# A hybrid RWKV-7, Hyena and PEER layer: the gate matrix of the dense tiles in three parts of 56, 16 and 56 blocks instead of four of 32, and eight first-layer blocks beside its first part

## The chip, the cores and the metric

One core of one Trainium2 chip runs the whole layer in one launch. The metric is the device time in microseconds (us), the median of repeated runs of the same program. In the text PE is TensorE, DVE is VectorE, ACT is ScalarE, POOL is GpSimd and SP is SyncE; "L1061" is line 1061 of the kernel before.

## The reference, cut to what matters

One layer of width D = 1024 on 128 context tokens and 512 latent tokens: modulation from `w_ada` (six parts), a mixer (combined projection `w_in`, low-rank "LoRA" products for decay, rate and gate, scans, long convolutions, `w_out`), and then PEER experts, all in float32:

```
def peer(h):                       # for all 640 tokens, 8 heads, top 16 of 16384 experts each
    q = (x @ peer_wq).reshape(T, 8, 2, 128)
    s = einsum('thpd,phkd->thpk', q, peer_keys)        # scores against 2 x 128 keys
    sv, si = top_k(s, 16)
    cand = sv[:, :, 0, :, None] + sv[:, :, 1, None, :]
    cidx = si[:, :, 0, :, None] * 128 + si[:, :, 1, None, :]
    top_s, pos = top_k(cand.reshape(T, 8, 256), 16)
    eidx = take_along_axis(cidx..., pos)               # 8 x 16 = 128 experts per token
    gate = softmax(top_s)
    act = gelu(einsum('cd,ced->ce', x, u_tab[eidx])) * gate
    return einsum('ce,ced->cd', act, v_tab[eidx])
x = x + gate2 * peer(h);  y = rmsnorm(x, final_norm)
```

`u_tab` and `v_tab` have 16384 rows of 1024 floats, 67 MB each.

## The kernel before, in words

**Start.** The weights `w_ada`, `w_in`, `w_out` and `peer_wq` come in chunks of 2 MB that SP issues into a ring of three slots (`WBUF` = 3), in the order of `WCH` (four `ada` chunks, one `in`, two `ada`, then mostly `in`). PE's modulation products (L544) take one `ada` chunk each. Five loads of the LoRA weights stand before the third chunk (`if n == 2`); what they bring is used by the LoRA products in the mixer, after the first `w_in` products.

**Tiles.** The 640 tokens are five tiles of 128. Each token of tile 0 (context) and of latent tiles 1 and 2 gets its 128 expert rows of `u` and of `v` by indirect DMA, one per slot (128 partitions of 1024 floats, 0.524 MB). Tile 0 is done before the stretch that the change is about. For tiles 1 and 2 there are `ROWS` = 512 such gathers, issued by POOL (L2213) into a ring of `RING` = 8 and consumed in order by DVE: a `u` row by one operation that forms the dot products (L2036), a `v` row by one that adds it to the sum (L2041). POOL waits until DVE has given a slot back.

**Dense tiles.** The last two latent tiles (`ND` = 256 tokens) are computed against all 16384 experts, in `ETILES` = 128 blocks of 128 experts. Per block i:

- SP loads `u` block i (three buffers) once `hidden(i - 3)` is done, and `v` block i (two buffers) once `back(i - 2)` is done, 0.524 MB each.
- PE `hidden(i)` (L1061, 16 records of 128x256): expert activations from the `u` block, into one of two PSUM banks.
- ACT takes the gelu of it to one of four buffers `sgel` (L1389).
- DVE `weigh(i)` multiplies it by row i of the gate matrix (L2080).
- PE `back(i)` (L1072, 8 records of 128x512) adds its product with the `v` block to the output in PSUM.

**The gate matrix** `gmat` holds, for a block and a token, the gates of the 128 experts of the block. It is built from one-hot vectors, for 8 tokens at a time (a group; `GROUPS` = 32 groups per part), and for `QI` = 32 blocks at a time (a part; `NPART` = 4). For a group, DVE makes three arrays: `one_j` (L2068, 1024 bf16 elements a partition), `same_i` (L2071, 8 per block of the part) and `one_i` (L2073, 24 per block of the part). PE multiplies them, 24 matmuls (L1083), and ACT copies the result to `gmat` (L1397), which has two halves of 32 rows. One-hots and PSUM have two buffers. The first part stands before block 2's `hidden`; the groups of each further part are spread over the 28 steps after its predecessor's start, by `groups_by(i)`.

**Order.** Each engine runs its own list, written out by hand, with semaphores between them. PE's list:

```
hidden(0); hidden(1)
... transposes of the slots and gates of the dense tiles ...
for g in range(GROUPS): gate_group(g)
for i in range(2, ETILES):
    hidden(i); back(i - 2); the gate groups due by groups_by(i - 2)
```

DVE's step i is: `weigh(i)`, the one-hots due, a piece of the top-k of tile 1 or 2 (`FIRST_STEPS`: the first stage; `ROUTE_STEPS`: the routing, whose end releases that tile's gathers on POOL through `eid_ok`), and the gathered rows due by `rows_by(i)`: 400 over the steps 12 to 95, then 112 over the steps 95 to 126. After step 127 come the final sums and norms (`fin_*`).

**Ahead of block 0.** The top-k of the two dense tiles (t = 3 and 4) runs on DVE, with an exponential on ACT (`route_exp`) that waits for DVE's routing. ACT copies the tokens `h2` of the gathered tiles (L1380), and PE's transposes wait for those copies (L1049). PE then spreads the output gate `gate2` over the partitions (`spread`, L726; ACT's copy `g2bc`, L1382), which is used first when the final sums of the tiles are made (steps 104 and 108).

Of the kernel before, what the change touches and what calls it, by code (L numbers as in the profile page):

```python
# [71 lines left out]
QI = 32  # L72
GROUPS = ND // GRP
NPART = NKEY // QI
# [55 lines left out]
def program(nc, a, outs):  # L130
# [5 lines left out]
    with ExitStack() as ctx:  # L136
# [136 lines left out]
        gmat = at(SB - 2 * QI * ND, 2 * QI, ND)  # L273
# [7 lines left out]
        g2bc = pr(2, D)  # L281
        sc_a = at(g2bc.offset, 4, 2, NKEY)
# [10 lines left out]
        keyN = at(cand.offset, 2 * EXPH, NKEY)  # L293
        sv = tk(NLT, 2 * EXPH, TOPK)
# [25 lines left out]
        one_i = [half(hr(3 * QI * GRP // 2), 3, QI, GRP) for _ in range(2)]  # L320
        same_i = half(hr(QI * GRP // 2), 1, QI, GRP)
        iota8 = half(hr(P * GRP // 2), 1, P, GRP)
        slot5 = half(hr(5 * ND // 2), 5, 2, P)
        junk = hr(D).bitcast(mybir.dt.bfloat16).rearrange("p (a b) -> p a b", b=D)
# [5 lines left out]
        yo = [at(gmat.offset + (NT + 1 + t if t < 2 else QI * ND // D + t - 2) * D, D) for t in range(NT)]  # L330
# [39 lines left out]

        block = ctx.enter_context(nc.Block())
# [3 lines left out]
        def _(sp):  # L375
# [135 lines left out]
            for i in range(ETILES):  # L511
                if i + UB < ETILES:
                    sp.wait_ge(S("s_mm"), i + 1)
                    load_u(i + UB)
                if i >= 2 and i - 2 + VB < ETILES:
                    sp.wait_ge(S("v_mm"), i - 1)
                    load_v(i - 2 + VB)
                if i == 100:
                    sp.wait_ge(S("x_out"), 16)
                    sp.wait_ge(S("xc_out"), 16)  # L520
                    sp.wait_ge(S("a_ok"), (NPART - 1) * QI)
                    sp.dma_start(xr, spill).then_inc(S("ld_xr"), 16)
                    sp.dma_start(fnorm, a["final_norm"].partition_broadcast(P)).then_inc(S("ld_xr"), 16)
# [8 lines left out]
        def _(pe):  # L532
# [531 lines left out]
            def back(i):  # L1064
# [3 lines left out]
                if i == 0:  # L1068
                    pe.wait_ge(S("gate_ok"), 3)
                for r in range(2):  # L1070
                    for c in range(2):
                        m = pe.matmul(ps[:, 2 * r + c, :], sgel[:, i % SBUFS, P * r:P * r + P], vs[i % VB][:, 512 * c:512 * c + 512],  # L1072
# [3 lines left out]
            def gate_group(g):  # L1076

                pe.wait_ge(S("one_ok"), g + 1)
                if g >= 2:
                    pe.wait_ge(S("g_ev"), g - 1)  # L1080
                for c in range(GRP):
                    for k in range(3):
                        m = pe.matmul(ps[:, 6 + g % 2, QI * c:QI * c + QI], one_j[:, g % 2, :, c], one_i[g % 2][:, k, :, c],  # L1083
# [28 lines left out]
        def _(act):  # L1112
# [257 lines left out]
            for n in range(4 * EXPH):  # L1370
                q_out(n)
                for t in (3, 4):
                    if n == ROUTE_AT[t]:
                        route_exp(t - 1)
# [6 lines left out]
            act.wait_ge(S("gate_mm"), 3)  # L1381
            own.do(A(g2bc[:, :, :].rearrange("p c n -> p (c n)"), ps[:, 0:4, :].rearrange("p a b -> p (a b)"), ACT.Copy), S("gate_ok"))  # L1382

            def gelu_out(i):

                act.wait_ge(S("s_mm"), i + 1)
                if i >= SBUFS:
                    act.wait_ge(S("v_mm"), i - SBUFS + 1)
                A(sgel[:, i % SBUFS, :], ps[:, 4 + i % 2, 0:ND], ACT.Gelu).then_inc(S("gel_ok"), 1)  # L1389

            def gates_out(g):
# [3 lines left out]
                if q >= 2:  # L1395
                    act.wait_ge(S("a_ok"), QI * (q - 1))
                A(gmat[:, QI * (q % 2):QI * (q % 2) + QI, GRP * k:GRP * k + GRP], ps[:, 6 + g % 2, 0:QI * GRP].rearrange("p (t i) -> p i t", i=QI),  # L1397
                  ACT.Copy).then_inc(S("g_ev"), 1)

# [16 lines left out]
            for g in range(GROUPS):  # L1416
                gates_out(g)
            ng, ne, nr = 2, GROUPS, 4
            for i in range(ETILES):
                while ng < min(i + 3, ETILES):  # L1420
                    gelu_out(ng)
                    while ne < groups_by(ng - 2):
                        gates_out(ne)
                        ne += 1
                    ng += 1
# [21 lines left out]
        def _(dve):  # L1447
# [577 lines left out]
            def gather_row(n):  # L2025
# [9 lines left out]
                if e == 0:  # L2035
                    V.scalar_tensor_tensor(junk[:, m % 2, :], slot, 1.0, h2[:, 1 + t, :], ALU.mult, ALU.mult,  # L2036
# [24 lines left out]
            def one_hots(g):  # L2061
# [67 lines left out]
            dve.wait_ge(S("gate_ok"), 3)  # L2129
# [16 lines left out]
            for i in range(ETILES):  # L2146
# [10 lines left out]
                for k, t in enumerate((1, 2)):  # L2157
# [7 lines left out]
                    if i == lo:  # L2165
                        parts[t] = route_tile(t)
# [125 lines left out]
```

## Time and profile before

| | |
|---|---|
| median of the runs | 2684.29 us (2683.68, 2684.29, 2685.72) |
| profiled execution, its own time | 2703.06 us |
| its span, from first to last instruction | 2701.2 us |
| mean granted clock of TensorE | 0.933 of full speed |
| busy: PE | 2391.4 us (89%) |
| busy: PE weight loads | 1674.8 us (62%) |
| busy: DVE | 1794.5 us (66%) |
| busy: ACT | 495.1 us (18%) |
| busy: POOL | 937.1 us (35%) |
| read from HBM | 635.5 MB |

The profile is of one execution, and all times of the trace count from the start of its span. An engine's busy time says how much of the span it worked, not whether it set the pace; for that the span has to be taken stage by stage, and the waits in a stage read. A granted clock of 1 is 2.4 GHz, of 0.5 is 1.2 GHz; a mean between them says for what share of a stretch each held. A release behind `<-` names what ended the idle time before an instruction.

### The profile page before, as it was taken

The numbers are of one execution on the slowest core, as the hardware profiler recorded it, in microseconds if no ns is written. First come the engines' busy times: TensorE is split into PE (matmuls) and PEld (weight loads), VectorE is DVE, ScalarE is ACT, GpSimd is POOL, SyncE is SP. The second block draws the span as 40 slices with busy tenths as digits, with TensorE's granted clock in tenths as the row PEclk, the third lists the DMA queues.
The fourth block names the chain that finished last, engine by engine and source line by source line (L and its number), as shares of the span: only waits on it lengthen the run. The fifth ranks groups of instructions, "written<-read, shape, count | busy, mean of one in ns | idle before, by whom it ended". The sixth has DMA issues, their size and how long they took to land.

```text
span 2701.2 us, 43634 instructions
## 1 busy us (share of the span) xinstructions
PE 2391.4 (89%) x18034; PEld 1674.8 (62%) x18034; DVE 1794.5 (66%) x3466; ACT 495.1 (18%) x1002; POOL 937.1 (35%) x774
## 2 busy tenths in 40 slices
PE   5989978788788878999879899998999899998997
PEld 2545536667777766334468787775776567775664
DVE  0111253335677776577689795799899888886767
ACT  2111124224344332100122210100000100000101
POOL 0000000000144442155441000667766567765653
PEclk8999988998899998899999769999999899999999
DMA  9233031130166665287886013999999999999997
GB/s 299 94 131 118 5 135 41 56 103 2 47 227 188 218 197 180 86 313 251 309 329 227 17 48 129 346 406 384 409 407 395 337 409 392 409 407 411 409 409 301
DMA packets 199455, 647.01 MB, mean 240 GB/s; under 512 B 25222, under 2 KB 27142, under 8 KB 198298
## 3 DMA queue, kind: packets, MB, share of 16 engines
q0 software_dynamic: 110592, 402.70, 39.8%
q1 hardware_dynamic: 88666, 241.52, 24.2%
q8 instruction: 143, 2.34, 0.4%
q14 instruction: 54, 0.44, 0.0%
HBM read 635.50 MB, written 8.65 MB: 238 GB/s over the span
## 4 chain that ended last, share of the span: by engine, by line
PE 55%; DVE 14%; DMA 13%; issue 6%; POOL 5%; ACT 4%; another core or an unknown queue 1%; SPq 1%; DVEq 0%; POOLq 0%; ACTq 0%
DMA arena<-in_peer_v,arena 8%; PE ps L1061 7%; PE ps L595 7%; PE ps L1072 7%; PE ps L1083 5%; POOL arena L2213 4%; DMA arena<-in_peer_u,arena 3%; PE ps L1037 3%; PE ps L829 3%; PE ps L987 2%; PE ps L1002 2%; DVE arena L2041 2%; PE ps L597 2%; PE ps L835 1%; DMA arena<-in_w_in 1%
## 5 line engine op out<-in xcount | busy, mean ns | idle before, releaser
L1072 PE MATMUL ps<-arena 128*128 128x512 f32 x1024 | 473.3, 606 | 45.2 <-DVE arena L2080 40.5
L1061 PE MATMUL ps<-arena 128*128 128x256 f32 x2048 | 480.2, 388 | 1.6 <-issue 1.6
L2213 POOL DMA_INDIRECT arena<-in_peer_u,arena x256 | 339.7, 1327 | 380.3 <-DVE arena L1832 231.9
L1061 PEld LDWEIGHTS ps<-arena 128*128 128x128 f32 x2048 | 392.1, 195 | 70.8 <-issue 21.3
L2213 POOL DMA_INDIRECT arena<-in_peer_v,arena x256 | 306.2, 1196 | 193.8 <-DVE arena L2041 141.3
L2041 DVE SCALAR_TENSOR_TENSOR arena<-arena 128x1024 f32<-128x1024 f32 x252 | 316.1, 1284 | 83.9 <-DMA arena<-in_peer_v,arena 77.1
L2201 POOL DMA_INDIRECT arena<-in_peer_u,arena x128 | 147.5, 1153 | 614.6 <-DVE arena L1832 335.4
L1072 PEld LDWEIGHTS ps<-arena 128*128 128x128 f32 x1024 | 196.1, 194 | 252.2 <-issue 241.4
L2036 DVE SCALAR_TENSOR_TENSOR arena<-arena 128x1024 bf16<-128x1024 f32 x256 | 304.1, 1223 | 46.6 <-DMA arena<-in_peer_u,arena 41.1
L1083 PEld LDWEIGHTS ps<-arena 128*128 128x128 bf16 x3072 | 207.2, 157 | 51.0 <-issue 47.0
L1083 PE MATMUL ps<-arena 128*128 128x32 bf16 x3072 | 210.3, 243 | 4.3 <-DVE arena L2073 4.1
L595 PE MATMUL ps<-arena 128*128 128x512 f32 x384 | 182.9, 632 | 20.2 <-DMA arena<-in_w_in 17.9
L2201 POOL DMA_INDIRECT arena<-in_peer_v,arena x128 | 140.5, 1098 | 172.7 <-DVE arena L1869 137.2
L1500 DVE SCALAR_TENSOR_TENSOR arena<-ps,arena 128x504 f32<-128x504 f32 x48 | 35.7, 743 | 242.3 <-ACT arena L1159 241.4
L829 PE MATMUL ps<-arena 64*64 64x128 f32 x1920 | 189.0, 282 | 8.0 <-ACT arena L1289 7.1
L1865 DVE SCALAR_TENSOR_TENSOR arena<-arena 128x1024 bf16<-128x1024 f32 x128 | 154.3, 1223 | 57.2 <-DMA arena<-in_peer_u,arena 56.8
L1869 DVE SCALAR_TENSOR_TENSOR arena<-arena 128x1024 f32<-128x1024 f32 x126 | 155.8, 1284 | 1.6 <-DMA arena<-in_peer_v,arena 1.0
L1389 ACT ACTIVATE arena<-ps 128x256 f32<-128x256 f32 x128 | 48.9, 383 | 554.8 <-PE ps L1061 464.0
L595 PEld LDWEIGHTS ps<-arena 128*128 128x128 f32 x384 | 76.1, 204 | 112.7 <-issue 88.6
L1397 ACT ACTIVATE arena<-ps 128x256 f32<-128x256 f32 x128 | 49.1, 384 | 473.6 <-PE ps L1083 452.1
L2191 POOL MEMSET arena<- 128x1024 f32 x1 | 1.0, 951 | 372.5 <-PE ps L614 372.5
L829 PEld LDWEIGHTS ps<-arena 64*64 64x64 f32 x1920 | 108.5, 139 | 27.4 <-issue 15.3
(354 smaller groups left out, 3431.2 us busy)
## 6 DMA issues: line engine op xcount, KB each, us to landing
arena<-in_uT SPq DMA_DIRECT2D x128, 512.0 KB
arena<-in_peer_v SPq DMA_DIRECT2D x128, 512.0 KB
arena<-in_w_ada SPq DMA_DIRECT2D x12, 2048.0 KB, 18.1
arena<-in_peer_wq SPq DMA_DIRECT2D x12, 2048.0 KB, 9.5
arena<-in_w_in SPq DMA_DIRECT2D x6, 2048.0 KB, 8.1
arena<-in_w_out SPq DMA_DIRECT2D x4, 2048.0 KB, 8.0
arena<-in_peer_u,arena POOLq DMA_INDIRECT x384
arena<-in_peer_v,arena POOLq DMA_INDIRECT x384
```

Of the source, the lines that this page charges most:

```text
L595: pe.matmul(ps[:, n % 2, :], w[:, k, P * f:P * f + P], hT[:, k, LC:T], start=(k == 0), stop=(k == KD - 1))
L829: m = pe.matmul(xo[r, u, :, i, :], nT[r, :], zz[r, h // 2, 0:2, i, :], start=False, stop=(l == LEVELS - 1), skip_group_check=True)
L1037: m = pe.matmul(ps[:, n % 2, 0:ND], ring[slot_of["wq", j]][:, k, P * f:P * f + P], half[:, k, :], start=(k == 0), stop=(k == KD - 1))
L1061: m = pe.matmul(ps[:, 4 + i % 2, 0:ND], us[i % UB][:, k, :], hTd[:, k, :], start=(k == 0), stop=(k == KD - 1))
L1072: m = pe.matmul(ps[:, 2 * r + c, :], sgel[:, i % SBUFS, P * r:P * r + P], vs[i % VB][:, 512 * c:512 * c + 512], start=(i == 0), stop=(i == ...
L1083: m = pe.matmul(ps[:, 6 + g % 2, QI * c:QI * c + QI], one_j[:, g % 2, :, c], one_i[g % 2][:, k, :, c], start=(k == 0), stop=(k == 2))
L1865: m = V.scalar_tensor_tensor(junk_c[c % 2], slot, 1.0, h2_c, ALU.mult, ALU.mult, accum_out=dots_c[:, m:m + 1])
L1869: m = V.scalar_tensor_tensor(dst, slot, coef_c[:, m:m + 1], dst, ALU.mult, ALU.add)
L2036: V.scalar_tensor_tensor(junk[:, m % 2, :], slot, 1.0, h2[:, 1 + t, :], ALU.mult, ALU.mult, accum_out=dots[:, m:m + 1]).then_inc(S("g_used ...
L2041: V.scalar_tensor_tensor(acc[:, m % 2, :], slot, coef[:, m:m + 1], acc[:, m % 2, :], ALU.mult, ALU.add).then_inc(S("g_used"), 1)
L2201: pool.indirect_dma_start(gring_c[k], None, a[("peer_u", "peer_v")[e]][0], bass.IndirectOffsetOnAxis(ap=ids_c[:, m:m + 1], axis=0)).then_i ...
L2213: pool.indirect_dma_start(gring[:, n % RING, :], None, a[("peer_u", "peer_v")[e]][0], bass.IndirectOffsetOnAxis(ap=ids[:, t, m:m + 1], axi ...
```

## The change

- The gate matrix is built in three parts, of 56, 16 and 56 blocks, in a `gmat` of 72 rows. A group of the first and third part has 56-block one-hots, so 24 matmuls of 56 columns. The second part's groups are due one a step from step 18 on, the third part's 32 groups in the 15 steps from 55.
- `hidden(0)` and `hidden(1)` stand where they did; `hidden(2)` to `hidden(7)` stand among the groups of the first part, after groups 4, 9, 14, 19, 24 and 29, on PE and ACT alike. The first four gelu results stay in rows 56 to 59 of `gmat`, which the second part fills later. SP loads the first `u` blocks accordingly.
- The routing of tile 1 takes the steps 4 to 10 (before: 4 to 12), that of tile 2 the steps 44 to 54 (44 to 58). The gathered rows are due from step 10 on, 400 over 85 steps, and the last 112 over 28 steps instead of 31.
- The exponential of tile 4's routing stands behind ACT's `h2` copies. The spreads of `gate2` and their copies move from before block 0 to the steps 96 and 98.
- The LoRA loads stand before the ninth weight chunk instead of the third.
- Buffers move with it: the dot operation's full-size result goes over its ring slot (before: `junk`), `sc_a` to `cand`, `g2bc` and `yo` to rows of `gmat`. `xr` is loaded after 96 weighings, as before.

```
-QI = 32
-NPART = NKEY // QI
+PARTS = ((0, 56), (56, 16), (72, 56))
+GROWS = 72
+FRONT = 4
+AHEAD = FRONT + SBUFS
+AHEAD_AT = {4: 2, 9: 3, 14: 4, 19: 5, 24: 6, 29: 7}
 def rows_by(i):
-    return max(0, min(EARLY, (i - 12) * EARLY // 83)) + max(0, min(ROWS - EARLY, (i - 95) * (ROWS - EARLY) // 31))
+    return max(0, min(EARLY, (i - 10) * EARLY // 85)) + max(0, min(ROWS - EARLY, (i - 95) * (ROWS - EARLY) // 28))
 def groups_by(i):
-    return min(NPART * GROUPS, GROUPS + GROUPS * (i // QI) + min(GROUPS, (i % QI + 1) * 8 // 7))
+    if i < 56:
+        return GROUPS + max(0, min(GROUPS, i - 17))
+    return min(3 * GROUPS, 2 * GROUPS + (i - 55) * GROUPS // 15)
-ROUTE_STEPS = {1: (4, 12), 2: (44, 58)}
-ROUTE_AT = {3: 2 * EXPH + 10, 4: 2 * EXPH + 15}
+ROUTE_STEPS = {1: (4, 10), 2: (44, 54)}
+ROUTE_AT = 2 * EXPH + 10
...
+        def sg(i):
+            return front[:, i, :] if i < FRONT else sgel[:, i % SBUFS, :]
...
-                if n == 2:
+                if n == 8:
                     for d in range(2):
                         sp.dma_start(lora1[...])
...
-            for i in range(ETILES):
-                if i + UB < ETILES:
+            for i in range(AHEAD):
+                sp.wait_ge(S("s_mm"), i + 1)
+                load_u(i + UB)
+            for i in range(2, ETILES):
+                if AHEAD <= i < ETILES - UB:
                     sp.wait_ge(S("s_mm"), i + 1)
                     load_u(i + UB)
-                if i >= 2 and i - 2 + VB < ETILES:
+                if i - 2 + VB < ETILES:
                     sp.wait_ge(S("v_mm"), i - 1)
                     load_v(i - 2 + VB)
...
-            for c in range(2):
-                m = spread(40, c, 2 * c)
-            m.then_inc(S("gate_mm"), 1)
...
             for g in range(GROUPS):
                 gate_group(g)
+                if g in AHEAD_AT:
+                    hidden(AHEAD_AT[g])
             ng = GROUPS
             for i in range(2, ETILES):
-                hidden(i)
+                if i >= AHEAD:
+                    hidden(i)
                 back(i - 2)
                 while ng < groups_by(i - 2):
                     gate_group(ng)
                     ng += 1
+                if i in (96, 98):
+                    pe.wait_ge(S("g_ev"), 3 * GROUPS)
+                    pe.wait_ge(S("gate_ok"), 2 + (i - 96) // 2)
+                    spread(40, (i - 96) // 2, 6).then_inc(S("gate_mm"), 1)
...
-            act.wait_ge(S("gate_mm"), 3)
-            own.do(A(g2bc..., ps[:, 0:4, :]..., ACT.Copy), S("gate_ok"))
+            route_exp(3)
...
+                if q == 1:
+                    act.wait_ge(S("v_mm"), FRONT)
+                if q == 2:
+                    act.wait_ge(S("a_ok"), w)
...
-                dve.wait_ge(S("g_ev"), GROUPS * (i // QI + 1))
+                dve.wait_ge(S("g_ev"), GROUPS * (part_of(i) + 1))
```

## Rows read from the trace of the kernel before

**Rows 1.** The page: GB/s in 40 slices; the gathers' queue (packets, MB, share)
```profile
GB/s 299 94 131 118 5 135 41 56 103 2 47 227 188 218 197 180 86 313 251 309 329 227 17 48 129 346 406 384 409 407 395 337 409 392 409 407 411 409 409 301
...
q0 software_dynamic: 110592, 402.70, 39.8%
```

**Rows 2.** Stage table: stretch, length, busy PE PEld DVE ACT POOL, clock, DMA, GB/s
```profile
1535.00:1595.00 60.00, 58.28 (x785) 54.73 (x786) 51.87 (x126) 12.43 (x33) 0.00 (x0) 0.52 0.01 2
1764.60:2446.00 681.40, 653.53 (x3598) 463.35 (x3596) 606.69 (x1106) 61.16 (x156) 462.74 (x363) 0.98 1.01 396
2446.00:2680.70 234.70, 217.67 (x736) 139.51 (x736) 167.07 (x160) 19.33 (x40) 130.72 (x110) 0.99 1.02 407
1981.90:2117.10 135.20, 123.42 (x686) 85.63 (x687) 132.59 (x217) 10.73 (x28) 78.70 (x66) 0.95 0.96 373
2079.90:2220.00 140.10, 123.92 (x602) 83.93 (x601) 125.69 (x160) 12.36 (x28) 86.72 (x73) 0.93 0.96 369
```

**Rows 3.** Timeline of PE at the start: start, us, instruction, idle time and releaser
```profile
22.20 1.92 PE L544 MATMUL ps<-arena 128*32 128x512 f32 x16 [1.75 <-DMA arena<-in_w_ada]
...
35.28 3.64 PE L544 MATMUL ps<-arena 128*32 128x512 f32 x16 [10.17 <-DMA arena<-in_w_ada]
...
41.07 3.47 PE L544 MATMUL ps<-arena 128*32 128x512 f32 x16 [0.35 <-DVE arena L1477]
```

**Rows 4.** Timeline of PE, from the h2 transposes to the first groups
```profile
1518.26 1.97 PE L1049 MATMUL ps<-arena 128*128 128x128 f32 x8 [8.46 <-ACT arena L1380]
...
1520.02 4.79 PE L726 MATMUL ps<-arena 128*128 128x128 f32 x32
1524.64 7.07 PE L1061 MATMUL ps<-arena 128*128 128x256 f32 x32
1535.54 26.06 PE L1083 MATMUL ps<-arena 128*128 128x32 bf16 x384 [3.17 <-DVE arena L2073]
```

**Rows 5.** Timeline: one group's operations on DVE, and hidden(2) behind the first part
```profile
1560.98 0.69 DVE L2068 TENSOR_TENSOR arena<-arena 128x1024 bf16<-128x1024 bf16 x1
1561.59 0.28 DVE L2071 TENSOR_TENSOR arena<-arena 128x256 bf16<-128x256 bf16 x1
1561.91 0.56 DVE L2073 TENSOR_TENSOR arena<-arena 128x768 bf16<-128x768 bf16 x1
1562.38 0.68 DVE L2068 TENSOR_TENSOR arena<-arena 128x1024 bf16<-128x1024 bf16 x1
...
1588.49 6.36 PE L1061 MATMUL ps<-arena 128*128 128x256 f32 x16
```

**Rows 6.** Timeline of PE at block 8; then the chain of waits at block 3
```profile
1648.91 3.06 PE L1083 MATMUL ps<-arena 128*128 128x32 bf16 x48
1651.79 5.38 PE L1061 MATMUL ps<-arena 128*128 128x256 f32 x16
```
```profile
1599.83 3.51 PE ps L1061 x16
1603.33 3.43 PE ps L1072 x8
```

**Rows 7.** Stage table of tile 4's routing and of a first stage; the first gather
```profile
1491.10:1517.10 26.00, 18.07 (x99) 15.97 (x97) 25.30 (x87) 4.16 (x16) 0.00 (x0) 0.90 0.00 0
1590.90:1596.20 5.30, 5.30 (x16) 3.82 (x15) 5.16 (x34) 0.38 (x1) 0.00 (x0) 0.72 0.10 19
```
```profile
1683.14 1.12 POOL L2213 DMA_INDIRECT arena<-in_peer_u,arena  x1 [231.90 <-DVE arena L1832]
```

**Rows 8.** Timeline: the ninth gather, and five rows of v on DVE
```profile
1708.81 1.68 POOL L2213 DMA_INDIRECT arena<-in_peer_u,arena  x1 [15.48 <-DVE arena L2036]
...
2119.08 6.09 DVE L2041 SCALAR_TENSOR_TENSOR arena<-arena 128x1024 f32<-128x1024 f32 x5
```

**Rows 9.** Waits from 1524 to the end: who, for whom: us, times, longest
```profile
DVE arena L2068 <- PE ps L1083: 49.6, 28, 7.0
```

**Rows 10.** Timeline of PE: the last block's back product
```profile
2682.59 5.37 PE L1072 MATMUL ps<-arena 128*128 128x512 f32 x8 [3.51 <-DVE arena L2080]
```

More of the change, by code:

```diff
@@ L71 @@
 UB, VB, SBUFS, GRP = 3, 2, 4, 8
-QI = 32
 GROUPS = ND // GRP
-NPART = NKEY // QI
+PARTS = ((0, 56), (56, 16), (72, 56))
+GROWS = 72
+WIDEST = max(w for _, w in PARTS)
+FRONT = 4
+AHEAD = FRONT + SBUFS
+AHEAD_AT = {4: 2, 9: 3, 14: 4, 19: 5, 24: 6, 29: 7}
 ROWS = (GT - 1) * 2 * SLOTS
@@ L319, in program @@
         one_j = half(hr(2 * P * GRP // 2), 2, P, GRP)
-        one_i = [half(hr(3 * QI * GRP // 2), 3, QI, GRP) for _ in range(2)]
-        same_i = half(hr(QI * GRP // 2), 1, QI, GRP)
+        one_at = [hr(3 * WIDEST * GRP // 2).offset for _ in range(2)]
+        one_i = [[half(at(o, 3 * w * GRP // 2), 3, w, GRP) for o in one_at] for _, w in PARTS]
+        same_at = hr(WIDEST * GRP // 2).offset
+        same_i = [half(at(same_at, w * GRP // 2), 1, w, GRP) for _, w in PARTS]
         iota8 = half(hr(P * GRP // 2), 1, P, GRP)
         slot5 = half(hr(5 * ND // 2), 5, 2, P)
-        junk = hr(D).bitcast(mybir.dt.bfloat16).rearrange("p (a b) -> p a b", b=D)
         us = [at(x.offset + i * D, KD, P) for i in range(UB)]
@@ L329, in program @@
         fnorm = at(gmat.offset + NT * D, D)
-        yo = [at(gmat.offset + (NT + 1 + t if t < 2 else QI * ND // D + t - 2) * D, D) for t in range(NT)]
+        yo = [at(gmat.offset + n * D, D) for n in (6, 14, 7, 8, 9)]
+        g2bc = at(gmat.offset + 15 * D, 2, D)
+        front = gmat[:, 56:56 + FRONT, :]
         ring_at = SB - WBUF * KD * 512
@@ L1080, in gate_group @@
                     pe.wait_ge(S("g_ev"), g - 1)
+                w = PARTS[g // GROUPS][1]
                 for c in range(GRP):
                     for k in range(3):
-                        m = pe.matmul(ps[:, 6 + g % 2, QI * c:QI * c + QI], one_j[:, g % 2, :, c], one_i[g % 2][:, k, :, c],
+                        m = pe.matmul(ps[:, 6 + g % 2, w * c:w * c + w], one_j[:, g % 2, :, c], one_i[g // GROUPS][g % 2][:, k, :, c],
                                       start=(k == 0), stop=(k == 2))
@@ L1371, in _ @@
                 q_out(n)
-                for t in (3, 4):
-                    if n == ROUTE_AT[t]:
-                        route_exp(t - 1)
+                if n == ROUTE_AT:
+                    route_exp(2)
             sc_out(4 * EXPH - 1)
@@ L1380, in _ @@
                 own.do(A(h2[:, 1 + i // 2, 512 * (i % 2):512 * (i % 2) + 512], ps[:, 4 + i % 2, :], ACT.Copy), S("h2_ok"))
-            act.wait_ge(S("gate_mm"), 3)
-            own.do(A(g2bc[:, :, :].rearrange("p c n -> p (c n)"), ps[:, 0:4, :].rearrange("p a b -> p (a b)"), ACT.Copy), S("gate_ok"))
+            route_exp(3)
             def gelu_out(i):
                 act.wait_ge(S("s_mm"), i + 1)
-                if i >= SBUFS:
+                if i >= AHEAD:
                     act.wait_ge(S("v_mm"), i - SBUFS + 1)
-                A(sgel[:, i % SBUFS, :], ps[:, 4 + i % 2, 0:ND], ACT.Gelu).then_inc(S("gel_ok"), 1)
+                A(sg(i), ps[:, 4 + i % 2, 0:ND], ACT.Gelu).then_inc(S("gel_ok"), 1)
             def gates_out(g):
@@ L1394, in gates_out, with gate_out @@
                 q, k = divmod(g, GROUPS)
-                if q >= 2:
-                    act.wait_ge(S("a_ok"), QI * (q - 1))
-                A(gmat[:, QI * (q % 2):QI * (q % 2) + QI, GRP * k:GRP * k + GRP], ps[:, 6 + g % 2, 0:QI * GRP].rearrange("p (t i) -> p i t", i=QI),
+                lo, w = PARTS[q]
+                row = lo % GROWS
+                if q == 1:
+                    act.wait_ge(S("v_mm"), FRONT)
+                if q == 2:
+                    act.wait_ge(S("a_ok"), w)
+                A(gmat[:, row:row + w, GRP * k:GRP * k + GRP], ps[:, 6 + g % 2, 0:w * GRP].rearrange("p (t i) -> p i t", i=w),
                   ACT.Copy).then_inc(S("g_ev"), 1)
+            def gate_out(c):
+                act.wait_ge(S("gate_mm"), 3 + c)
+                own.do(A(g2bc[:, c, :], ps[:, 6:8, :].rearrange("p a b -> p (a b)"), ACT.Copy), S("gate_ok"))
             def fin_square(t):
@@ L2035, in gather_row @@
                 if e == 0:
-                    V.scalar_tensor_tensor(junk[:, m % 2, :], slot, 1.0, h2[:, 1 + t, :], ALU.mult, ALU.mult,
+                    V.scalar_tensor_tensor(slot.bitcast(mybir.dt.bfloat16)[:, 0:D], slot, 1.0, h2[:, 1 + t, :], ALU.mult, ALU.mult,
                                            accum_out=dots[:, m:m + 1]).then_inc(S("g_used"), 1)
@@ L2165, in _ @@
                     if i == lo:
+                        rown.settle()
                         parts[t] = route_tile(t)
```

32 lines of the change are left out of this document (19 added, 13 removed).

## The prediction

> **What bounds the kernel now.** The page's slices come first: from the 26th on they move about 350 to 410 GB/s, most of them 409, while those from the 23rd to the 25th move 17 to 129 [rows 1]. The stage table splits that end [rows 2]; its edges are DVE's weighings of a block (the records of line 2080, counted). Between those of block 20 (1764.6) and block 95 (2446.0) DMA moves 396 GB/s, PE is busy 653.5 of 681.4 us and DVE 606.7. From 2446.0 to the last gathered row DMA moves 407 GB/s. So the last 1000 us are bound by bytes, with PE and DVE close behind. What comes before them is a chain in which DMA is almost idle: 1535 to 1595 moves 2 GB/s, with TensorE's clock at 0.52, that is mostly 1.2 GHz [rows 2]. A microsecond saved ahead of the first gather at 1683.14 [rows 7] starts the byte-bound stretch earlier; one of PE saved inside it saves nothing unless PE was the one that was late.
>
> **The start: the five LoRA loads go from before the third weight chunk to before the ninth.** PE waits 10.17 us for the third `w_ada` chunk, to 35.28, because SP issues it behind them [rows 3]. Without them it follows the second chunk, which was there at 22.2. A chunk is 2.1 MB, 5.1 us at 409 GB/s, so it lands at about 27.3. The fourth needs the slot of the first, long free then, and lands at 32.5; PE began on it at 41.07 [rows 3]. That is 8.5 us at the fourth chunk; I take 8, since PE idles twice there and may run it at the half clock. What follows, to the scores, is a chain that shifts as it stands. The loads now queue behind the second `w_in` chunk, for which PE waits too, but behind it in the same queue: 0 (at worst their 1.6 MB share with it, 4 us). **-8** (bounds -9 and -3).
>
> **Between scores and gate matrix.** PE idles 8.46 us for ACT's first copy of `h2`, which stands behind the exponential of tile 4's routing, then runs the 32 matmul records of the two `g2bc` spreads (4.79 us), then `hidden(0)` and `hidden(1)` (7.07), and the first group starts at 1535.54 [rows 4]. After the change the exponential stands behind the copies and the spreads are gone from here. The copies and transposes run at 1510 to 1513 and the two blocks to 1520, beside the routing, whose end on DVE (the exponential waits for it at 1517.1 [rows 7]) is then no longer what they wait for. From the end of `hidden(1)` to the first group the index transposes, ACT's copies and `split_gates` take the 3.8 us of now, or a little more, as ACT loads its gelu table there: 1524.3 instead of 1535.5. **-11** (bounds -12 and -7). The spreads come back at blocks 96 and 98, where PE has slack under the bytes: 0.
>
> **The first part of the gate matrix.** Now its 32 groups take 53.0 us (1535.5 to 1588.5), 1.63 each on PE (26.06 us for 384 matmuls) at the half clock [rows 4, 5]. DVE's three one-hot operations start 0.61, 0.32 and 0.47 us apart; they take 0.69, 0.28 and 0.56 us for 1024, 256 and 768 elements, 0.53 ns an element [rows 5]. With 56 blocks they have 1024, 448 and 1344: 0.61 + 0.42 + 0.78 = 1.81 us a group, 58 in all. On PE a group becomes 24 matmuls of 56 columns, which no row shows. From below it is the 32-column group at full clock, 1.53 us [rows 6], from above that in proportion to the columns, 2.7. I take 1.5 at full and up to 1.8 at half clock: 32 columns took 1.53 and 1.63 at the two clocks, so it is not the columns that they wait for. The Trainium skill, in "TensorE: Matmul & The Clock Gate", Back-to-back issue gap, prices 1 to 64 columns alike, by which 56 columns cost what 32 do; no run here has 56, and by the upper bound the first and the third part would cost PE some 37 us more each.
>
> Six `hidden` blocks now stand among these groups, one after every fifth. Behind 3.06 us of groups alone the block at 1651.79 took 5.38 us instead of 3.51, and the one behind the whole part 6.36 [rows 4, 5, 6]: groups bring the clock down, and a block behind them starts at 1.2 GHz. Each of the six has 9 us of groups before it, so I take 6.1 each, 36.6 in all; at full clock they would be 21. The opening is 58 + 36.6, less 1.6 that DVE gets ahead: 93 us, from 1524.3 to 1617. **+40 on the opening, +29 at its end.**
>
> **From there to the first gather.** Now 94.6 us (1588.5 to 1683.1), paced by PE steps of 3.51 + 3.43 + 1.5 = 8.4 us [rows 6], since every step holds a hidden block, a back block and a group that DVE's one-hots wait for. After the change PE has no groups before step 18 and only back blocks for steps 2 to 7, so DVE sets the pace: 1 us to the first weighing, four steps of 0.33 for the weighing and 5.2 for the first stage of four score rows (22.1), then the routing, 26.0 us when nothing disturbs it [rows 7]. Its heavy operations come in steps 8 and 9. Step 8 needs `hidden(8)`: weighing 4, two backs, one hidden, 23.4 + 10.4 = 34 us; from there DVE's step 8 takes 12 and step 9 six. **52 us**: the first gather at 1669.5, not 1683.1, -13.6.
>
> **The byte-bound stretch.** A row and a block of u or v are 0.524 MB each (402.7 MB are 768 gathers [rows 1]). Now DVE frees the first slot of the ring of 8 only 25.7 us after the first gather (1708.81); POOL stands 15.48 us for it [rows 7, 8]. After the change rows are due from step 11, and 42 before step 20; with 20 blocks of u and v that is 32.5 MB, 79.5 us at 409 GB/s, and 6 for landing and coupling: block 20 at 1755 (now 1764.6). Steps 20 to 95 hold 6.71 transfers each against 6.82: 8.58 us, 643.8 in all, against 655. Now they take 681.4, 26 over: 6.5 in steps 24 to 31 (9.54 each), 13 in 44 to 57 (135.2 us, DVE busy 132.6 [rows 2]), 7 spread. A row costs DVE 1.22 us (five in 6.09 [rows 8]). After:
> - 24 to 31: DVE has 5.74 rows + 0.33 + 1.25 (a 16-block group) + 1.72 (first stage: what 9.54 leaves now) = 9.04: +3.7.
> - 44 to 54: DVE 63.2 rows + 3.6 + 7.5 + 26 + 1 = 101.3 against 94.4: +6.9.
> - 55 to 69: the third part's 32 groups in 15 steps. PE 6.94 + 2.13 x 1.5 = 10.1; DVE 5.74 + 0.33 + 2.13 x 1.81 = 9.9. I take 10.3: +25.8.
> - spread: +7.
>
> That is 687.2, so block 95 at 2442 against 2446. The fourth part's groups, 1.5 us on PE and 1.4 on DVE each, leave engines that wait for bytes there: 0. From 95 on 112 rows, 56 blocks and 3.1 MB of residual are 91.2 MB, 223 us, + 4 as now (234.7 for 94.3 MB [rows 2]): last row at 2669, not 2680.7. The rows now end at step 123. Behind them stand, on PE alone, back(124), hidden(127) and three backs, 4 x 3.43 + 3.51 + 1.4 = 18.6, then the 13.2 us that follow the last back now [rows 10]: 2700.8. Against 2701.2: **-0.4**. So the 13.6 us ahead of the gather and the fuller start behind it are nearly all given back, to the crowded third part and the longer tail.
>
> **Sum.** -8 - 0.4: the span goes from 2701.2 to 2692.8, the profiled execution from 2703.06 to 2694.7. The median of the runs is 2684.29, 18.8 lower; the difference carried over unchanged gives **2676**.
>
> **Rivals.** (a) *The clock stays up in the opening.* For it: 56 columns stream 1.75 times as long as 32 in a group. Against it: the two blocks of rows 5 and 6. Then the six blocks cost 3.5 each and all 15 us are saved ahead of the gather: 2661. [...]
> (b) *The third part crowds out the rows; slower than before.* In steps 55 to 69 PE takes a group only when DVE has made it, and DVE makes one only when PE has taken the one two before; each has 10 us of work a step. Now DVE waits 28 times for PE's groups, up to 7.0 us [rows 9]. If the two alternate, one group's 1.5 + 1.8 us no longer overlap, a step is up to 12.2 us and DMA runs at under 330 GB/s. From 1.3 us a step over my 10.3 the saving is gone; at 11.7 (+21) it is 2697. For it: in 2079.9 to 2220 steps are 9.34 us at 369 GB/s [rows 2] with half the groups. Against it: DVE's stretch 1981.9 to 2117.1, busy 132.6 of 135.2, shows no such waiting.
> (c) *The start doesn't carry.* If the LoRA loads hold up `w_in`, or a later load takes the 8 us back, the dense part's nothing is left: 2684.
>
> **Chances.** Forecast 0.40, (a) 0.15, (b) 0.33, (c) 0.12. 0.2% (5.4 us) is about what a measurement can tell. The forecast's own range is 2667 to 2685: 0.27 faster, 0.11 same, 0.02 slower. (a) is 0.15 faster; (b) 0.26 slower, 0.07 same; (c) 0.06 faster, 0.06 same. Together 0.48, 0.24, 0.28. The range runs from below (a) to above (b)'s middle: 2655 to 2701.
>
> **What would show it.** In the profile after: the third `w_ada` wait ending near 27; the first group at 1516; six `hidden` blocks of 5.2 to 6.9 us among groups, and a clock near 0.6 there; DVE's groups 1.8 us apart; the first gather near 1661; steps 55 to 69 at 10.3 us with DMA near 340 GB/s; 70 to 95 at 8.6 with DMA at 409; 32 us from the last row to the end. It is wrong if 56-column groups take much over 1.5 us at full clock, if the six blocks take 3.5, if steps of the third part pass 11.5, or if the spread losses of 20 to 95 go or double, since I carried them over.

## The result, and the profile after

The kernel after takes 2766.5 us (median of 4 runs, 2763.5 to 2767.8), the kernel before beside it 2685.0: a ratio of 1.031, 95% interval 1.029 to 1.032. A later set of runs, with the kernel before at 2703.9, gave 1.030 (1.027 to 1.033). It is 3% slower, where 0.3% faster was forecast, and lies outside the forecast's range of 2655 to 2701 us. Two of the ten executions of e3 below took 3432 and 3918 us, and its ratio is that of the other eight. The profiled execution took 2763.5 us, its span is 2761.6.

Two lines of the page after, the granted clock and the GB/s by slices of 69 us:

```profile
PEclk9999979889899998999998689999999889999999
GB/s 270 118 180 61 61 114 2 89 65 2 128 223 192 221 222 46 309 265 261 369 276 23 25 83 359 409 370 404 409 358 328 248 246 345 409 409 411 408 408 241
```

Against [rows 1] one hole is new: the 31st to 33rd slices move 328, 248 and 246 GB/s, where they moved 395, 337 and 409 before. The stage table after, with the columns of [rows 2], cut at the first group, the first weighing, the first gather, the blocks 20, 55, 73 and 95, and the start of the last gathered row's operation:

```profile
1497.84:1614.20 116.36, 115.71 (x864) 109.47 (x864) 58.11 (x97) 19.83 (x38) 0.00 (x0) 0.68 0.09 28
1614.20:1666.50 52.30, 46.60 (x129) 25.37 (x130) 49.67 (x227) 1.15 (x3) 0.02 (x1) 0.94 0.34 115
1666.50:1753.40 86.90, 83.06 (x320) 54.62 (x318) 57.11 (x103) 7.65 (x16) 59.43 (x49) 0.98 1.01 398
1753.40:2069.70 316.30, 292.55 (x1548) 201.79 (x1548) 290.25 (x596) 24.81 (x69) 202.23 (x165) 0.98 0.99 388
2069.70:2304.30 234.60, 234.60 (x1215) 184.74 (x1213) 166.20 (x239) 24.37 (x50) 107.04 (x84) 0.88 0.74 271
2304.30:2496.10 191.80, 161.40 (x545) 101.70 (x544) 135.17 (x223) 9.76 (x24) 135.42 (x105) 0.98 1.03 409
2496.10:2727.50 231.40, 207.62 (x704) 131.25 (x703) 163.76 (x156) 19.97 (x40) 125.92 (x111) 0.99 1.01 401
```

In the fifth stage PE is busy 234.60 of 234.60 us and DVE 166: these are the steps with the third part's groups. Before, the blocks 55 to 73 took

```profile
2079.90:2248.60 168.70, 152.52 (x770) 104.91 (x769) 149.51 (x205) 15.04 (x35) 105.70 (x85) 0.93 0.96 370
```

The timeline of PE shows what the opening and that stage consist of (start, us, instruction):

```profile
1497.84 13.20 PE L1096 MATMUL ps<-arena 128*128 128x56 bf16 x120 [4.25 <-DVE arena L2106]
1510.86 5.35 PE L1075 MATMUL ps<-arena 128*128 128x256 f32 x16
1516.05 13.14 PE L1096 MATMUL ps<-arena 128*128 128x56 bf16 x120
...
2134.02 3.60 PE L1084 MATMUL ps<-arena 128*128 128x512 f32 x8
2137.45 5.35 PE L1096 MATMUL ps<-arena 128*128 128x56 bf16 x48
2142.62 5.21 PE L1075 MATMUL ps<-arena 128*128 128x256 f32 x16
```

L1096 is the gate group (L1083 before), L1075 `hidden` and L1084 `back`. Five groups of 56 columns take 13.20 us, 2.64 each, where 32 columns took 1.63 [rows 4] and I had put 1.5 to 1.8. Two of them in a step take 5.35. Stage rows of single stretches: groups alone in the third part, the `hidden` block behind them, and groups alone in the opening:

```profile
2124.00:2128.90 4.90, 4.90 (x48) 4.90 (x47) 1.85 (x3) 0.55 (x1) 1.55 (x2) 0.98 1.00 388
2129.00:2131.50 2.50, 2.50 (x8) 2.06 (x7) 2.27 (x4) 0.54 (x1) 0.00 (x0) 0.50 0.90 365
1498.00:1510.80 12.80, 12.80 (x120) 12.80 (x120) 8.86 (x15) 2.19 (x4) 0.00 (x0) 0.50 0.00 1
```

The granted clock is 0.98, 0.50 and 0.50. The first and the third row are groups alone, so a matmul of 56 columns costs about 110 ns at 1.2 and at 2.4 GHz alike. It is not TensorE's own speed that it waits for. The second row belongs to a `hidden` block behind a pair of groups, which takes 5.2 us, where one behind a single group of the second part takes 3.70. That part's groups, with 16 columns, are the cheap ones (1.58 us for 24 matmuls):

```profile
1757.45 1.58 PE L1096 MATMUL ps<-arena 128*128 128x16 bf16 x24
1758.88 3.70 PE L1075 MATMUL ps<-arena 128*128 128x256 f32 x16
```

### The profile page after: what moved, and what is told of

It is laid out like the page before. It is cut to its first block, busy times and chain, and to the rows that moved or that the text cites. A ratio compares the mean times of both kernels' runs of the same rounds, so it can differ in the third digit from the quotient of the medians.

```text
span 2761.6 us, 41938 instructions
## 1 busy us (share of the span) xinstructions
PE 2439.6 (88%) x17266; PEld 1707.7 (62%) x17266; DVE 1773.6 (64%) x3370; ACT 491.8 (18%) x971; POOL 919.2 (33%) x774
## 4 chain that ended last, share of the span: by engine, by line
PE 45%; DMA 20%; DVE 18%; issue 7%; POOL 5%; ACT 3%; SPq 0%; DVEq 0%; POOLq 0%; ACTq 0%
DMA arena<-in_peer_v,arena 9%; DMA arena<-in_peer_u,arena 9%; PE ps L613 7%; PE ps L1096 6%; PE ps L1075 6%; PE ps L1084 4%; POOL arena L2248 4%; PE ps L1005 2%; PE ps L1020 2%; PE ps L847 2%; PE ps L615 2%; DVE arena L1743 1%; DVE arena L2073 1%; POOL arena L2236 1%; DVE arena L1901 1%
## 5 line engine op out<-in xcount | busy, mean ns | idle before, releaser
L1084 PE MATMUL ps<-arena 128*128 128x512 f32 x1024 | 480.0, 614 | 89.8 <-DVE arena L2113 88.3
L1075 PE MATMUL ps<-arena 128*128 128x256 f32 x2048 | 502.2, 402 | 0.7 <-issue 0.7
L2248 POOL DMA_INDIRECT arena<-in_peer_u,arena x256 | 331.0, 1293 | 421.3 <-DVE arena L1864 239.5
L1075 PEld LDWEIGHTS ps<-arena 128*128 128x128 f32 x2048 | 412.7, 204 | 90.8 <-issue 34.9
L1084 PEld LDWEIGHTS ps<-arena 128*128 128x128 f32 x1024 | 194.1, 196 | 315.6 <-issue 311.2
L2248 POOL DMA_INDIRECT arena<-in_peer_v,arena x256 | 299.0, 1168 | 237.7 <-DVE arena L2073 180.6
L2068 DVE SCALAR_TENSOR_TENSOR arena<-arena 128x1024 bf16<-128x1024 f32 x256 | 308.1, 1223 | 89.3 <-DMA arena<-in_peer_u,arena 87.6
L2236 POOL DMA_INDIRECT arena<-in_peer_u,arena x128 | 146.1, 1142 | 602.9 <-DVE arena L1864 335.6
L1096 PEld LDWEIGHTS ps<-arena 128*128 128x128 bf16 x2304 | 219.7, 153 | 29.6 <-issue 29.1
L1096 PE MATMUL ps<-arena 128*128 128x56 bf16 (+1 forms) x2304 | 220.6, 263 | 4.2 <-DVE arena L2106 4.2
L613 PE MATMUL ps<-arena 128*128 128x512 f32 x384 | 183.0, 633 | 19.8 <-DMA arena<-in_w_in 17.6
L2236 POOL DMA_INDIRECT arena<-in_peer_v,arena x128 | 140.0, 1093 | 170.3 <-DVE arena L1901 134.8
L1407 ACT ACTIVATE arena<-ps 128x256 f32<-128x256 f32 x128 | 49.0, 384 | 758.2 <-PE ps L1075 758.2
L613 PEld LDWEIGHTS ps<-arena 128*128 128x128 f32 x384 | 76.2, 204 | 112.4 <-issue 88.7
L2100 DVE TENSOR_TENSOR arena<-arena 128x1024 bf16<-128x1024 bf16 x96 | 66.3, 690 | 108.0 <-PE ps L1096 107.9
L847 PEld LDWEIGHTS ps<-arena 64*64 64x64 f32 x1920 | 106.8, 139 | 23.0 <-ACT arena L1306 12.6
## 6 DMA issues: line engine op xcount, KB each, us to landing
arena<-in_peer_wq SPq DMA_DIRECT2D x12, 2048.0 KB, 10.1
```

Source lines behind the costliest of these rows:

```text
L613: pe.matmul(ps[:, n % 2, :], w[:, k, P * f:P * f + P], hT[:, k, LC:T], start=(k == 0), stop=(k == KD - 1))
L847: m = pe.matmul(xo[r, u, :, i, :], nT[r, :], zz[r, h // 2, 0:2, i, :], start=False, stop=(l == LEVELS - 1), skip_group_check=True)
L1075: m = pe.matmul(ps[:, 4 + i % 2, 0:ND], us[i % UB][:, k, :], hTd[:, k, :], start=(k == 0), stop=(k == KD - 1))
L1084: m = pe.matmul(ps[:, 2 * r + c, :], sg(i)[:, P * r:P * r + P], vs[i % VB][:, 512 * c:512 * c + 512], start=(i == 0), stop=(i == ETILES - 1))
L1096: m = pe.matmul(ps[:, 6 + g % 2, w * c:w * c + w], one_j[:, g % 2, :, c], one_i[g // GROUPS][g % 2][:, k, :, c], start=(k == 0), stop=(k = ...
L2068: V.scalar_tensor_tensor(slot.bitcast(mybir.dt.bfloat16)[:, 0:D], slot, 1.0, h2[:, 1 + t, :], ALU.mult, ALU.mult, accum_out=dots[:, m:m + ...
```

## The experiments

Two theories stood after this. **Step**: the elements of the one-hot arrays that a matmul reads lie 16 bytes apart (8 tokens of 2 bytes, `[:, k, :, c]`), and TensorE waits for them, about 1.95 ns a column; narrow groups hide it under a floor. **Columns**: 56 columns cost that much however they lie. A third, **clock**, was already weak by the rows above.

**The cost by itself.** A bench of matmuls alone, 96 of each kind in the groups' pattern, and then the one-hot operations on VectorE.

```
pe.matmul(ps[...], weights with a step of 16, 8, 4 or 2 bytes, 16..64 columns with such a step)
```

> A bench and not the layer: the outputs are zeros, and TensorE runs stretches of 96 bf16 matmuls in the pattern of the gate groups (own 128x128 weights each, three to an accumulation), with 16 to 64 columns, and with elements of the moving operand and of the weights 16, 8, 4 or 2 bytes apart; VectorE then runs the one-hot operations in several layouts. Theory A (step): the 56 columns cost 2.6 us a group because the moving elements are 16 bytes apart, some 1.95 ns a column, and narrower ones are hidden under a floor. Then 16 bytes apart gives 62 ns a matmul for 16 columns, 64 for 32, 78 for 40, 94 for 48, 109 for 56, 125 for 64; with 8, 4 or 2 bytes 56 and 64 columns take the floor, 60 to 66 ns; the step of the weights moves nothing. Theory B (columns): 56 columns take 109 ns whatever the step. Theory C (clock): the cost follows the granted clock of the stretch, about 65 ns at 2.4 GHz and 109 or more at 1.2.

> A second bench like the first (outputs zeros), to part the two operands: the first showed 62 ns a matmul with the weights in steps of 16 bytes whatever the moving step, 57 with both at 8, and 27 with both adjacent. Theory A: each operand has a time of its own, and the longer one sets the pace. Then with adjacent weights 56 moving columns take about 104 ns at 16 bytes and 27 to 30 at 8, 4 and 2 bytes, and 32 columns at 16 bytes about 62; with adjacent moving columns the weights alone give 62 ns at 16 bytes, about 57 at 8, and 27 to 57 at 4 bytes. Theory B: the times add up; then 8-byte moving columns with adjacent weights take well over 30 ns.

The timelines of PE in the first bench: 16, 32, 48, 56 and 64 columns with both operands in steps of 16 bytes, then 56 columns with the moving operand in steps of 8 (weights 16), and with both adjacent:

```profile
17.80 5.90 PE L222 MATMUL ps<-arena 128*128 128x16 bf16 x96
36.85 6.34 PE L226 MATMUL ps<-arena 128*128 128x32 bf16 x96
...
75.30 9.12 PE L234 MATMUL ps<-arena 128*128 128x48 bf16 x96
96.20 10.72 PE L238 MATMUL ps<-arena 128*128 128x56 bf16 x96
119.39 11.81 PE L242 MATMUL ps<-arena 128*128 128x64 bf16 x96
143.47 5.99 PE L246 MATMUL ps<-arena 128*128 128x56 bf16 x96
...
230.38 2.64 PE L266 MATMUL ps<-arena 128*128 128x56 bf16 x96
```

and in the second: 56 columns in steps of 16, 8, 4 bytes with adjacent weights, then adjacent columns with weights in steps of 16 and of 8, and last 32 columns in steps of 16 with adjacent weights:

```profile
17.90 9.89 PE L222 MATMUL ps<-arena 128*128 128x56 bf16 x96
40.67 5.26 PE L226 MATMUL ps<-arena 128*128 128x56 bf16 x96
56.13 2.68 PE L230 MATMUL ps<-arena 128*128 128x56 bf16 x96
...
81.90 5.94 PE L238 MATMUL ps<-arena 128*128 128x56 bf16 x96
98.06 3.36 PE L242 MATMUL ps<-arena 128*128 128x56 bf16 x96
...
140.62 5.92 PE L254 MATMUL ps<-arena 128*128 128x32 bf16 x96
```

Divided by 96, ns a matmul:

| step in bytes | 16 | 8 | 4 | 2 |
|---|---|---|---|---|
| 56 moving columns, adjacent weights | 103 | 55 | 28 | 27.5 |
| 128 weight columns, 56 adjacent moving | 62 | 35 | 27.6 | 27.5 |

Each operand has a time of its own: at 16 bytes about 1.84 ns a moving column and 0.48 ns a weight column, at 8 bytes about half of that. The longer one decides, and does not add to the other; below both there is a floor of 27 ns. This is a little too simple: with both at 16 bytes 16, 32, 48, 56 and 64 columns take 61, 66, 95, 112 and 123 ns, which is 4 ns more than the longer operand alone for 32 columns (62) and 9 more for 56 (103). The kernel before sat at the corner: at 32 columns the moving operand takes 62 ns, as the weights do.

Theory "step" had the moving operand right and the floor wrong. Its 60 to 66 ns are no floor of TensorE but the time of the weights at 16 bytes, of which it had said that their step moves nothing. For the weights at 8 bytes I had expected 57 ns; they take 35, and it was the moving operand that took the 57 of the first bench.

The Trainium skill has this in "SBUF — State Buffer", Door 1: The DMA port swizzle: memory lines of 16 bytes, and a penalty for each access that goes to a new line. The bench agrees for steps of 16 bytes (103 ns against 27.5 adjacent). It does not agree that up to there the step is free for 2-byte elements: 56 moving columns in steps of 8 bytes take 55 ns, in steps of 4 bytes 28.

**The moving operand read as adjacent elements**, in the kernel after (correct gate values are what this version leaves out; its instructions and waits are the same):

```
-  one_j[:, g % 2, :, c], one_i[g // GROUPS][g % 2][:, k, :, c],
+  one_j[:, g % 2, :, c], one_i[g // GROUPS][g % 2].rearrange("p k w c -> p k (w c)")[:, k, w * c:w * c + w],
```

> The kernel after, with the gate groups' moving operand read as adjacent elements from the same buffers (so the gate values are not those of the layer; all instructions and waits stay). Theory A (step): a group falls from 2.6 to about 1.55 us on TensorE; the opening is again paced by VectorE, 95 us instead of 116, the steps of the third part take about 10.5 us instead of 13.7, and the kernel comes to about 2692 us. Theory B (columns) and theory C (clock): the groups stay at 2.6 us and the kernel at 2766.

2690.1 us beside 2696.2 for the kernel before, ratio 0.996 (0.995 to 0.998). Its stages of opening and third part:

```profile
1507.77:1593.80 86.03, 80.58 (x864) 73.12 (x864) 56.75 (x97) 19.73 (x38) 0.00 (x0) 0.74 0.13 38
2050.40:2233.00 182.60, 178.61 (x1217) 133.67 (x1215) 164.47 (x237) 26.32 (x54) 110.22 (x85) 0.98 0.93 348
```

The same instructions take 86.0 instead of 116.4 us and 182.6 instead of 234.6, 82 us together, as much as the kernel had lost (81.5). The granted clock of the third part is 0.98 instead of 0.88:

```profile
2086.18 3.05 PE L1096 MATMUL ps<-arena 128*128 128x56 bf16 x48
2089.07 3.70 PE L1075 MATMUL ps<-arena 128*128 128x256 f32 x16
```

Two groups take 3.05 us and the block behind them 3.70, not 5.2. So in the third part the slow reads cost twice: once by themselves, and once by the half clock that the next `hidden` gets. In the opening they cost only once: there the blocks among the groups take 5.1 to 5.3 us in e1 too.

**The layer's own results with a step of 8 bytes:** tokens by halves of four, `one_i` in two operations.

```
+  one_i ... .rearrange("p (h k i c) -> p h k i c", h=2, k=3, c=4)
-  one_j[:, g % 2, :, c], one_i[...][g % 2][:, k, :, c]
+  one_j[:, g % 2, c // 4, :, c % 4], one_i[...][g % 2][:, c // 4, k, :, c % 4]
```

> The kernel after with the one-hot arrays laid out by halves of four tokens, so that TensorE reads both operands of a gate group in steps of 8 bytes instead of 16; VectorE makes each one_i in two operations of half the size. All results are the layer's. Theory A (step): as with adjacent elements, about 1.55 us a group on TensorE, less 0.1 us a group for the second operation on VectorE: 2690 to 2700 us. Theory B (columns): 2766 or a little more.

2690.0 beside 2696.2 (0.998, 0.996 to 1.000). A group takes 1.49 us, the third part's stage 178.9. The theory "columns" is out by both e1 and e3. The theory "clock" is out by the first and third row of single stretches above. This version keeps the layer's results and comes out level with the kernel before.

**The kernel after again**, on the chip of the last runs:

> The kernel after, unchanged, on the chip of these runs, for a comparison beside them. The kernel before ran at 2696 to 2700 us in the last two sets and at 2685 in the first; if the ratio holds, the kernel after takes 3.1% more than it here too, 2779 to 2783 us; if the place where before was slower is one that the change avoids, 2766.

2780.7 beside 2703.9, ratio 1.030. From its first group to its end are 1262.1 us (1263.8 in the first profile), but its first group starts at 1514.0 and not at 1497.8. So 16 us of the early start in the first profile were the execution's and not the change's.

**The kernel before again:**

> The kernel before, unchanged, for a second profile of it. Theory 1: the 18.8 us by which the profiled execution of before stood above the median of its runs were spent at one place, the stretch from 966 to 1048 us (tile 0's gathers), where the profile after is 13 to 15 us shorter although the change touches nothing there; then this profile differs from the first by several us there and by less than 3 us in each other stage. Theory 2: they are the cost of taking a profile and fall everywhere, and then the stages agree within 2 us, this one too.

Its span is 2697.1. Between 966 and 1063 us it is 3.5 us shorter than the first profile; every other stage agrees within 2. From the first to the 128th of tile 0's gathers (709.3 to 1134.4 us in the first profile of before) it takes 421.5 us instead of 425.1; the first profile of after takes 411.8, its repetition 431.3, and e2 429.1. That stretch, which the change does not touch, varies between executions, of one kernel too. Theory 2 is out, and theory 1 holds for the place only: 3.5 us there do not make 18.8. What else lay between the profile of before and its median, and what causes the variation, stays open; it was not tried.

**The start edits alone**, with four parts of 32 (LoRA loads, exponential, spreads of `gate2`):

```
-  if n == 2:          # LoRA loads
+  if n == 8:
...
+  route_exp(3)        # behind the h2 copies; spreads at the steps 96 and 98
```

> The kernel before with only the edits ahead of the gate matrix: LoRA loads before the ninth chunk, the exponential of tile 4 behind the h2 copies, the gate2 spreads at the steps 96 and 98. If these carry through to the end: LoRA 8, the score stage 7, the h2 wait 9.5, the spreads 3, together 24 to 27 us, so 2658 to 2661 us. If the byte-bound stretch takes them back: 2677 to 2685.

2679.4 beside 2696.2, ratio 0.993 (0.990 to 0.995): 17 to 20 us faster. The LoRA loads give 8.2 us up to the second `w_in` product (58.86 against 67.08); from the last score to the first group it is 12.6 us shorter. The time lies where I had expected it if the bytes took the start back, but they do not: from the first group to the end e2 takes 1159.3 us, before 1165.7 and 1163.9. What is missing from the 24 to 27 us that I had expected are the 7 us in the score stage that I read from the profile after. They do not come back, in this kernel or in e1: they were the execution's too.

**The blocks beside the first part**, taken back into the loop (on e3):

```
-AHEAD_AT = {4: 2, 9: 3, 14: 4, 19: 5, 24: 6, 29: 7}
+AHEAD_AT = {}          # hidden(i) before back(i - 2) for all i >= 2
```

> The kernel e3, with hidden(2) to hidden(7) back in the loop, each before its own step, and not among the groups of the first part. If they are free there, since VectorE paces the groups, their 3.5 us each come back to the steps: the first gather about 15 us later, 2700 to 2705 us. If they cost their full 5.3 us at the half clock among the groups, the opening shrinks by 30 us and the eight steps behind it grow by as much or less: 2685 to 2692, no difference to be told.

2682.9 beside 2699.9, ratio 0.994 (0.992 to 0.996), where e3 has 0.998. From the first group to the first gather it takes 125.7 us, e3 138.1. In e3 each block takes about 5.3 us, as it begins at the half clock, and DVE, with one-hots made two ahead at most, stands meanwhile; in the loop they take 3.6. The six blocks ahead cost 12 us.

**The last rows over 31 steps again** (on e3):

```
-(i - 95) * (ROWS - EARLY) // 28
+(i - 95) * (ROWS - EARLY) // 31
```

> The kernel e3 (8-byte steps), with the last 112 gathered rows spread over 31 steps again instead of 28. If the tail behind the last row costs what the stage sum says, it shrinks from about 34 to 21 us, of which the bytes take some back: 6 to 9 us less than e3, 2681 to 2684 us. If the end is bound by bytes alone: no change, 2690.

2685.0 beside 2699.9, ratio 0.994 (0.993 to 0.996). From the first group to the end 1169.5 us, against 1175.9 in e3. The tail behind the last row's end is 20.5 us instead of 32.6, as costed, and the bytes take 6 of these 12 us back.

**A version that beats both:** e2 with the routing of tile 1 packed, then variants.

```
-ROUTE_STEPS = {1: (4, 12), 2: (44, 58)}
+ROUTE_STEPS = {1: (4, 9), 2: (44, 58)}       # b1; rows_by from step 9, 400 over 86 steps
+ROUTE_STEPS = {1: (4, 9), 2: (38, 59)}       # b2
+part 2's groups: (i - 8) * 8 // 5            # b3, on b1
```

> The kernel e2 (start edits, four parts of 32), with the routing of tile 1 in the steps 4 to 9 instead of 4 to 12 and the gathered rows due from step 9. In these steps TensorE sets the pace, 8.4 us a step, and VectorE has 5.5 us of work; with 7.4 us it still fits. Then the first gather comes three steps earlier, 25 us, and as the stretch behind it is bound by bytes most of it should reach the end: 2655 to 2665 us. If TensorE's blocks and groups up to step 32 bound that stretch and not the bytes: 2675 to 2680, as e2.

> The kernel b1, with the routing of tile 2 in the steps 38 to 59 instead of 44 to 58, three pieces a step instead of four and eight at the end. If VectorE is over the bytes only in those steps, spreading gives back up to 8 us: 2655 to 2660. If the whole stretch from 32 to 60 is bound by VectorE's total work: no change, 2663.

> The kernel b1, with the second part's groups due in the steps 8 to 28 (8 in 5 steps) instead of 0 to 28. TensorE's steps before the first gather fall from 8.4 to 6.9 us and VectorE's by 1.8, so the gather comes 10 to 14 us earlier; TensorE's sum up to step 28 stays. If the bytes bound what follows, the end comes 5 to 12 us earlier, 2651 to 2658; if TensorE does, no change or slower, 2663 to 2668.

b1: 2663.4 beside 2699.9, ratio 0.987 (0.983 to 0.990). First group to first gather: 136.0 us instead of 145.3 in e2, so 9 us and not 25. The stage row of its blocks 4 to 8:

```profile
1599.80:1641.90 42.10, 42.10 (x255) 30.37 (x254) 24.16 (x101) 3.83 (x10) 0.00 (x0) 1.00 0.35 116
```

PE is busy throughout and DVE for 24.16 us: PE paces these steps, as expected, but e2 has its last piece of routing in step 11, and b1 in step 9, so there were two steps to win and not three, and DVE meets PE's groups in each of them. First group to end: 1147.9 instead of 1159.3. b2: 0.985 (0.981 to 0.988), 1142.9 us; not told apart from b1 by the runs, 5 us less in the profiles. b3: 0.988 (0.985 to 0.991), not told apart from b1 either. The first gather comes 112.7 us after the first group, 23 us sooner than in b1 and not the 10 to 14 that I had expected; but the steps 8 to 20 take 119.6 us instead of 103.7, with PE busy throughout, and the steps 20 to 32 122.7 instead of 109.7. First group to end is 1157.7 us, 10 more than in b1: what PE saved before the gather it has to do behind it, and the earlier gather alone brings nothing here.

## Why the prediction was wrong

The step that failed is the price of a 56-column group on PE: "I take 1.5 at full and up to 1.8 at half clock: 32 columns took 1.53 and 1.63 at the two clocks, so it is not the columns that they wait for." It measured 2.64 (and 2.67 in pairs), near the upper bound of 2.7 that the text had set in proportion to the columns. The inference was wrong in form: that 32 columns cost the same at both clocks shows that the clock does not set their price, and says nothing of the columns. Equal times at two clocks should have pointed to something outside TensorE, such as the reads. The price for 1 to 64 columns is one and the same in the Trainium skill ("TensorE: Matmul & The Clock Gate", Back-to-back issue gap). In the benches that holds nearly for adjacent elements (26.7, 26.6, 27.5 and 30.8 ns for 16, 32, 56 and 64 columns) and not for moving elements in steps of 16 bytes. The code shows the step (`one_i[...][:, k, :, c]`), and the prediction did not look at it.

A second term fell with it. The third part's step counted `hidden` and `back` at full clock, 6.94 us together; behind two slow groups `hidden` alone took 5.2 instead of 3.7. The prediction had given this half clock to the opening only, though the block of [rows 6] behind two groups showed it.

By stages, from the first group on, in us:

| stage | forecast | after | e1 (adjacent) |
|---|---|---|---|
| first group to first weighing | 93 | 116.4 | 86.0 |
| to the first gather | 52 | 52.3 | 52.3 |
| to block 20 | 85.5 | 86.9 | 87.1 |
| 20 to 55 | 314 | 316.3 | 317.2 |
| 55 to 73 | 182 | 234.6 | 182.6 |
| 73 to 95 | 191 | 191.8 | 191.1 |
| 95 to the last row's end, and the tail | 227 + 32 | 232.7 + 32.8 | 264.9 in all |
| sum | 1176.6 | 1263.8 | 1181.2 |

(The forecast's stages from 20 on are its 8.58 us a step with its losses put where it put them.) All terms but the two with wide groups hold within 6 us, 11 in sum: 23 us were missed in the opening and 52 in the third part. With that one price as assumed, the forecast was 0.997 of before, and e1, which makes the price so, measured 0.996. That they agree so closely is in part luck: e1's opening is 7 us shorter than forecast and the rest 12 longer.

- **LoRA loads, -8:** right, 8.2 in e2; the third `w_ada` wait ends at 27.9 in the profile after (27.3 forecast).
- **Scores to gate matrix, -11:** right: -12.6 in e2 and, for the kernel after, -9.2 in the first profile and -12.2 in the second.
- **Six blocks at 6.1:** 4.8 to 6.4, on average 5.6, at a granted clock of 0.56 to 0.76. Rival (a), a clock that stays up, is out. What the forecast did not ask is whether they are cheaper in the loop; by e5 they are, by 12 us in all.
- **DVE's groups 1.8 apart:** true in e3 (1.87), hidden in the kernel after, where PE sets the pace. The waits from 1490 us to the end have, for [rows 9],

```profile
DVE arena L2100 <- PE ps L1096: 107.9, 53, 9.2
```

  L2100 being the one-hot operation that L2068 was.
- **Rival (b)** named the right place and the right side, at a price that was too low: it put 12.2 us on a step, from PE and DVE alternating. The 18 steps from block 55 take 13.0 on average, and PE alone fills them. The mechanism was not alternation; with fast groups (e1) the steps are 10.1, as the forecast had it. One of its figures is also wrong in itself: the saving of 8 us is gone from some 0.55 us a step over 10.3 (15 steps), not from 1.3.
- **Rival (c)**, a start that does not carry: out by e2.
- **From span to median:** "the difference carried over unchanged" was an error of its own. It took 18.8 us off; the profile after lies 3 us below its median. It made the forecast too low by some 20 us in absolute time, while the ratio is not touched.

## What to carry to other kernels

Before a matmul is made wider, look at the byte step of both operands: here, with 2-byte elements, 16 bytes cost 1.84 ns a moving column and 0.48 a weight column, which 32 columns hid and 56 did not. A price that does not move with TensorE's clock, as these 110 ns, was set by something else; find what it is before it is scaled. When a bound is far from the value taken (here 75 us), and a bench or a look at the access pattern can decide it, the wider bound belongs in the forecast as a rival of its own.

## What the runs showed of the hardware

- A bf16 matmul of 16 to 56 columns with own 128x128 weights takes 27 ns when both operands are adjacent, less than half of what the kernel's groups take at their best (62 to 66).
- Where TensorE's matmuls waited for strided reads, the granted clock fell to 0.50 for the block behind two groups (5.2 us instead of 3.7), although PE counts as busy throughout; with adjacent moving elements, in steps that are otherwise the same, the stage keeps 0.98. This does not hold for every such stretch. In the benches the 24 f32 matmuls behind 9.89 us of 56 columns in steps of 16 bytes take 13.1 us, but behind 5.99 us of 56 columns in steps of 8 bytes, with weights in steps of 16, they take 10.55, as behind adjacent ones.
- On VectorE the layout that gives TensorE adjacent elements has its price: `one_i` of 1344 elements takes 1.56 us with the token's value constant along the inner dimension, against 0.86 as it stands, and an operation of `one_j`'s 1024 elements 1.23 against 0.69 (there the bench multiplies in the one and compares in the other, so the layout's share of that difference is not shown). Halves of four tokens keep the fast form (0.51 us for 672).
